# Norms of the gated delta rule: sums in four column groups, one rsqrt, then a spread from single rows

## What is computed

```python
def l2_normalize(x, eps=L2_EPS):
    xf = x.astype(F32)
    return xf * lax.rsqrt(jnp.sum(xf * xf, axis=-1, keepdims=True) + eps)

# in hybrid_mixer
gq, gk, gv = (to_heads(t, GDN_HEADS, GDN_HEAD_DIM) for t in jnp.split(gdn_qkv, 3, axis=-1))
gq, gk = l2_normalize(gq), l2_normalize(gk)
# in gated_delta_rule
q = q * (Dk ** -0.5)
```

## Time and profile before

| | us |
|---|---|
| median of 3 runs | 1766.57 |
| the three runs | 1766.11, 1766.57, 1770.18 |
| profiled execution, its own time | 1765.99 |
| its span in the trace | 1764.1 |

### The profile page before, as it was taken

One profiled execution on the slowest core, in us unless ns is written; L12 is line 12 of the kernel. 1 busy time (PEld: TensorE's weight loads), 2 busy tenths in 40 slices (PEclk: granted clock), 3 DMA queues, 4 the chain that ended last, 5 costly groups with the idle time before them and its releaser, 6 DMA issues.

```text
span 1764.1 us, 35889 instructions
## 1 busy us (share of the span) xinstructions
PE 1751.2 (99%) x15412; PEld 1660.0 (94%) x15412; DVE 1199.3 (68%) x1861; ACT 959.8 (54%) x1508; POOL 69.8 (4%) x32
## 2 busy tenths in 40 slices
PE   9999999999999999999999999999999999999999
PEld 8999998899999999999988899999989989889999
DVE  7775666765766666866577566766674668865676
ACT  6544567455644454545566466444564565655662
POOL 0000011400000000000113100000000000000000
PEclk9999999999999999999999999999999999999999
DMA  9665543333565665555533344556645635556332
GB/s 359 192 193 197 175 153 120 109 118 123 179 193 193 206 207 195 192 193 178 169 130 109 98 155 149 196 192 192 193 166 168 227 108 168 180 167 250 122 120 96
DMA packets 84461, 301.24 MB, mean 171 GB/s; under 512 B 9168, under 2 KB 11728, under 8 KB 84176
## 3 DMA queue, kind: packets, MB, share of 16 engines
q1 hardware_dynamic: 84160, 298.70, 50.9%
q10 hardware_dynamic: 144, 0.26, 0.1%
HBM read 297.88 MB, written 1.05 MB: 169 GB/s over the span
## 4 chain that ended last, share of the span: by engine, by line
PE 94%; DVE 3%; ACT 1%; issue 1%; DMA 0%; DVEq 0%; ACTq 0%
PE bank L408 22%; PE bank L413 21%; PE bank L415 21%; PE bank L433 3%; PE bank L429 3%; PE bank L432 3%; PE bank L748 2%; DVE w_lo L1677 1%; PE bank L675 1%; PE bank L1086 1%; PE bank L679 1%; PE bank L678 1%; PE bank L1137 1%; PE bank L908 1%; PE bank L925 1%; PE bank L1107 1%
## 5 line engine op out<-in xcount | busy, mean ns | idle before, releaser
L1677 DVE TENSOR_TENSOR w_lo<-ring,w_hi 128x1024 fp32r<-128x1024 f32 x541 | 651.0, 1240 | 94.9 <-ACT w_hi L1208 89.8
L1208 ACT ACTIVATE w_hi<-ring 128x1024 fp32r<-128x1024 f32 x541 | 561.8, 1057 | 237.9 <-PE bank L408 185.1
L408 PE MATMUL bank<-xs,w_hi 128*128 128x256 f32 x2160 | 601.5, 278 | 0.7 <-DVE w_lo L1677 0.7
L413 PE MATMUL bank<-xs,w_hi 128*128 128x256 f32 x2165 | 597.4, 276 | 0.0
L415 PE MATMUL bank<-xs,w_lo 128*128 128x256 f32 x2160 | 597.3, 277 | 0.0
L408 PEld LDWEIGHTS bank<-xs,w_hi 128*128 128x128 f32 x2160 | 405.8, 188 | 2.4 <-issue 2.0
L413 PEld LDWEIGHTS bank<-xs,w_hi 128*128 128x128 f32 x2165 | 406.2, 188 | 0.2
L415 PEld LDWEIGHTS bank<-xs,w_lo 128*128 128x128 f32 x2160 | 405.6, 188 | 0.0
L415 PE MATMUL bank<-a,w_lo 128*128 128x256 f32 x704 | 194.3, 276 | 0.0
L408 PE MATMUL bank<-a,w_hi 128*128 128x256 f32 x704 | 194.3, 276 | 0.0
L413 PE MATMUL bank<-a,w_hi 128*128 128x256 f32 x704 | 194.3, 276 | 0.0
(11 more groups left out here) (416 smaller groups left out, 2956.9 us busy)
## 6 DMA issues: line engine op xcount, KB each, us to landing
ring<-in_w SPq DMA_DIRECT2D x557, 512.0 KB, 3.4
arena<-in_mem SPq DMA_DIRECT2D x2, 1024.0 KB, 8.5
const<-in_const SPq DMA_DIRECT2D x1, 1199.0 KB, 6.8
out<-h SPq DMA_DIRECT2D x3, 256.0 KB, 2.5
dec_par<-in_dec SPq DMA_DIRECT2D x1, 695.0 KB, 11.1
h<-in_x SPq DMA_DIRECT2D x1, 512.0 KB, 7.9
h<-in_x SPq DMA_DIRECT2D x1, 260.0 KB, 4.1
ring<-in_w ACTq DMA_DIRECT2D x1, 256.0 KB, 4.3
```

What stands on the lines that cost most here:

```text
L408: last = nc.tensor.matmul(o, wh, hi(x, k0 + k), start=k == 0, stop=False, skip_group_check=True)
L413: nc.tensor.matmul(o[:, c:c + piece], wh, lo(x, k0 + k)[:, c:c + piece], start=False, stop=False, skip_group_check=True)
L1208: nc.scalar.activation(w_hi[:, s * UNIT:(s + 1) * UNIT], ring[:, u % RU, :], AF.Copy).then_inc(sems("w_hi"), 1)
L1677: nc.vector.tensor_tensor(w_lo[:, r * UNIT:(r + 1) * UNIT], ring[:, r, :], w_hi[:, s * UNIT:(s + 1) * UNIT].bitcast(F32), ALU.subtract).th ...
```

## The change

The four sums now use 32 columns of the array each (`ones[:, 0:32]`) and write four groups of 32 partitions of one bank, 6. So partitions 32j to 32j+31 hold the sum of pair j, and one signal follows the last of them. One `rsqrt` (a Ln and an Exp on 128 x 512) makes all four results in `sq[:, 0:2]`. After `keys(1)`, TensorE waits for it and spreads each pair's row over all 128 partitions, with a stationary operand of one row (`ones[32j:32j+1, :]`) and partition 32j of `sq` as the moving row, into the four banks that held the sums before. VectorE's `normed` takes its factors from these banks and not from `sq`. The waits of the v transposes and of `brow` now go by `qkn`, since `normed` is now what reads those banks last.

```diff
                 keys(3)
+                pe.e.wait_ge(*pe.need('l_sq', 2))
+                pe.e.wait_ge(*pe.need('gcol', 1))
+                pe.e.wait_ge(*pe.need('o_out', 4))
                 for j in range(4):
-                    pe.e.wait_ge(*pe.need('l_sq', j // 2 + 1))
-                    if j == 0:
-                        pe.e.wait_ge(*pe.need('gcol', 1))
-                        pe.e.wait_ge(*pe.need('o_out', 4))
-                    if j >= 2:
-                        pe.e.wait_ge(*pe.need('os_out', j - 1))
-                    nc.tensor.matmul(bank[NORM_BANKS[j]][:, :], ones, sq[:, 2 * j:2 * j + 2, :], start=True, stop=True,
-                        skip_group_check=True).then_inc(*pe.tell('l_full'))
+                    last = nc.tensor.matmul(bank[6][32 * j:32 * j + 32, :], ones[:, 0:32], sq[:, 2 * j:2 * j + 2, :],
+                        start=True, stop=True, skip_group_check=True)
+                last.then_inc(*pe.tell('l_full'))
                 keys(1)
+                pe.e.wait_ge(*pe.need('l_rstd', 1))
+                pe.e.wait_ge(*pe.need('os_out', 2))
+                for j in range(4):
+                    nc.tensor.matmul(bank[NORM_BANKS[j]][:, :], ones[32 * j:32 * j + 1, :], sq[32 * j:32 * j + 1, 0:2, :],
+                        start=True, stop=True, skip_group_check=True).then_inc(*pe.tell('l_full'))
                 pe.e.wait_ge(*pe.need('ys', 3))
-                pe.e.wait_ge(*pe.need('l_ln', 2))
+                pe.e.wait_ge(*pe.need('qkn', 2))
...
                 for c in range(2):
-                    pe.e.wait_ge(*pe.need('l_ln', 3 + c))
+                    pe.e.wait_ge(*pe.need('qkn', 3 + c))
                     nc.tensor.matmul(bank[4 + c][:, :], ones, bm[:, 4 * c:4 * c + 4, :], start=True, stop=True,
...
-                for j in range(4):
-                    a.e.wait_ge(*a.need('l_full', j + 1))
-                    rsqrt(a, sq[:, 2 * j:2 * j + 2, :], tiles(bank[NORM_BANKS[j]][:, :], 2), 1.0, "l_rstd", "l_ln")
+                a.e.wait_ge(*a.need('l_full', 1))
+                rsqrt(a, sq[:, 0:2, :], tiles(bank[6][:, :], 2), 1.0, "l_rstd", "l_ln")
...
                 def normed(j):
-                    d.e.wait_ge(*d.need('l_rstd', j + 1))
+                    d.e.wait_ge(*d.need('l_full', j + 2))
                     y = yc[:, 2 * j:2 * j + 2, :]
                     nc.vector.scalar_tensor_tensor(out=y, in0=y, scalar=P ** (-0.5) if j < 2 else 1.0,
-                        in1=sq[:, 2 * j:2 * j + 2, :], op0=ALU.mult, op1=ALU.mult).then_inc(*d.tell('qkn'))
+                        in1=tiles(bank[NORM_BANKS[j]][:, :], 2), op0=ALU.mult, op1=ALU.mult).then_inc(*d.tell('qkn'))
```

## The result

The changed kernel took 1770.4 us as the median of 20 runs (1765.66 to 1775.66), the kernel before, beside it, 1765.81 (1764.16 to 1772.18). The ratio is 1.0026, 95% interval 1.0016 to 1.0036. That is slower, by a little less than the 0.3% named above, and inside the range; the forecast of 1767.9 was 2.5 too low. Two further series of the changed kernel gave 1768.66 and 1768.77 against 1766.59 and 1766.43, so +2.1 and +2.3.

What follows compares the result with a forecast made beforehand. TensorE, busy 99% of the span, bounds the kernel. Per layer 2.41 us go out of the sums, while spread 1.07 and waits 0.52 and 1.48 come in: +0.66, twice +1.3, so 1767.9 us; 8-in-10 range 1764.7 to 1771.4.

Steps and rivals of the forecast that it cites:

- the 0.3% named above: 5.3 us, about what a measurement of this kernel can tell from no change; a result within it got 0.87.
- The sums: TensorE's four sums in each layer: four column groups run side by side, 1.02 us in place of 3.43.
- The rsqrt: ScalarE's Ln still starts behind the table load at 302.73; TensorE, done earlier, waits 0.52 us for the result.
- The spread: New TensorE work after the wait for ScalarE: four one-row groups run side by side, 1.07 us in each layer.
- The products and the second pause: VectorE's four products with the norms: the v transposes wait for the second, so TensorE idles 1.48 us.
- The mark: TensorE's start of `keys(1)` behind the k transposes, 309.00 before: 0.66 us late in each layer, delaying everything behind it.
- rival 3: Solve: four more matmuls per layer move the 1.44 us pause; if it and its clock fall vanish, 1764.8; 14%.
- rival 2: Around the spread: new pauses make the clock fall, 1.7 us each time; 1769.6 with one, 1771.3 with both; 17%.
- Rival 1: Sums and spread: groups go one after the other, +3.43 us in each layer, 1773.5 in all; 9%.
- Rival 4: Norms: both TensorE waits are hidden and the saved work comes back, 1.34 us gained per layer, 1763.9; 4%.

## Why the prediction was right, and where it was short

- **The sums**: predicted 1.02, measured 1.00 (in the second series' trace `keys` takes over 1.0 after the start). Four column groups run side by side.
- **The rsqrt**: Ln starts with the end of the table load, at 302.15, as it did. The wait for it was to be 0.52; the timeline shows 0.19 beyond the modelled end of the last matmul, 0.36 by the starts.
- **The spread**: predicted 1.07, measured 1.07 to the next start where something is queued behind it (304.27 to 305.34) and 1.14 with its tail. Four row groups of one row run side by side; in one group they take 3.6. Where the prediction counts two more changes between the full array and groups, there are four: into and out of the sums, and into and out of the spread. The measured times, 1.00 and 1.07, hold whatever these cost.
- **The products and the second pause**: predicted 1.48, measured 1.45.
- **The mark**: predicted +0.66, measured +0.59 in each layer, so +1.2 of the forecast +1.3.
- **The whole at an undisturbed clock**: +1.64 (error 0.17), so 0.46 beyond the two marks. Where this arises stays open. The pauses inside the solve's groups, which rival 3 named, are not the answer: before they are 1.44 and 0.51 in the first layer and 0.69 and 0.87 in the second, 3.51 together; in the changed kernel's undisturbed execution 1.29, 0.38, 1.40 and 0.47, 3.54 together. They moved among themselves:

```profile
351.81 0.71 PE L748 MATMUL bank<-arena 32*32 32x32 f32 x59 [0.51 <-issue]
974.78 0.67 PE L748 MATMUL bank<-arena 32*32 32x32 f32 x54 [0.69 <-issue]
982.29 0.26 PE L748 MATMUL bank<-arena 32*32 32x32 f32 x6 [0.87 <-issue]
...
338.28 0.50 PE L751 MATMUL bank<-arena 32*32 32x32 f32 x35 [1.29 <-issue]
350.17 0.80 PE L751 MATMUL bank<-arena 32*32 32x32 f32 x66 [0.38 <-issue]
974.55 0.82 PE L751 MATMUL bank<-arena 32*32 32x32 f32 x69 [1.40 <-issue]
981.59 0.38 PE L751 MATMUL bank<-arena 32*32 32x32 f32 x21 [0.47 <-issue]
```

- **The clock**: this is the step that failed. The forecast took it for a rival with 0.17, to be had or not, and argued against it that falls are rare and that full-array work stands right before and behind. But falls are not rare: the kernel before has a mean clock of 0.99865 over 83 runs, or about 1.4 falls in each execution. One profile, with its single fall, had shown no more than one draw; that one of the three runs of before took 1770.18 was a sign of it. The full-array work that stands right before and behind did not keep the clock up: it was down behind the norms in 3 of the 6 places profiled. With the change falls are more frequent, by 1.2 us on average over three series (0.0008 by 1.52 for each 0.001) and by more in the first. It is a term of the sum, to be counted with its average, and not a case that either comes or doesn't. With it the forecast would have been 1767.9 + 1.2 = 1769.1, and the measured medians were 1770.4, 1768.7 and 1768.8. So the mechanism of the timeline was right, and the size of the forecast was too small. That the first median is inside the range is due to rival 2, which drew its upper end, and in part to luck: the kernel before was 0.76 faster beside it than the 1766.57 the forecast was added to. Had it stood there, the same +4.6 would have given 1771.2, at the edge of the range.
- **Rival 1** is refuted for this kernel by the sums and the spread; its price was right in size: with the work done in one group and all rows, `keys` starts at 311.92 where the sums start at 299.28, 12.64 against the 12.69 of its working. **Rival 3** did not come: the pause in the solve stayed (1.29), and that the fall behind it is missing in the undisturbed execution goes with the clock, since a version with a filled pause has it again at 338.3. **Rival 4** did not come: the table load and the chain behind it stayed where they were. The version with both pauses filled shows what it takes to get that gain: 1.0 us in each layer by its timeline (12.09 - 11.08), 0.7 by the level at clock 1.000, where rival 4 had 1.34.

## What to carry to other kernels

Cutting this piece of the bounding engine's work by two thirds (3.43 to 1.0) gained nothing here, since the step behind it was held by another engine's list; before such a change, ask what other work stands ready for the time that comes free, and move it there in the same edit. What holds the step here is ScalarE's table load, which ends at 302.15; starting it earlier was not tried. The step that was split in two, with a round trip to another engine in each half, got a pause for each trip (0.2 and 1.45 us). Where runs differ by a few us, compare executions at the same mean granted clock: that made a difference of 1.6 us visible under a scatter of 10.

## What the runs showed of the hardware

- Four float32 matmuls on 512 columns take 3.43 us on the whole array, 1.00 in four column groups with 128 rows each, and 1.07 in four row groups of one row each; four of one row in the same row group take 3.62 at the full clock (first layer, 305.60 to 309.22). What counts for the time is whether each has a group of its own, not how many rows it uses.
- Where TensorE was busy for some 3.6 us with products of one row, the granted clock went to 0.50 in all three traces, at both places: for 3.4 us in the first layer, and for 6.8 us, from within the spread, in the second. With 128 rows it did not, at either place of the one trace (medians 1777.89 against 1771.92).
- The clock also fell where a pause of 1.45 us came after 1.1 us of such products, in 3 of 6 places; with 2.65 us in both layers of the one trace. The same program has a mean clock between 0.994 and 1.000 from one execution to the next, 1.52 us for each step of 0.001 by the fit.
